# A fifteenth weight buffer loaded behind the gathers, a shorter router, and a first expert tile copied by two engines

## The chip, the cores and the metric

The kernel runs on one core of a Trainium2 chip, from one launch. The metric is the device time of one execution, in microseconds (us). The engines are TensorE (PE in the profile), VectorE (DVE), ScalarE (ACT), GpSimd (POOL) and SyncE (SP). SP and POOL issue the DMA transfers that are spoken of here. All tensors are float32.

## The reference, cut to what matters

One layer of a decoder over 520 tokens (512 of a prompt, 8 of a decoding batch), model width 1024. Four token mixers, gates and an output projection give `hres`; then a mixture of experts follows, and the change is there:

```python
def hier_moe(x, rg_w, rg_b, re_w, re_b, w1, w3, w2):
    pg = softmax(t @ rg_w + rg_b)              # 4 groups
    pg_top, g_idx = top_k(pg, 1)               # the best group
    le = (t @ re_w + re_b).reshape(-1, 4, 4)   # 4 experts in each
    le_sel = einsum('ng,nge->ne', g_oh, le)
    e_val, e_idx = top_k(le_sel, 2)            # the two best experts in it
    wts = softmax(e_val) * pg_top
    h = silu(t @ w1[e]) * (t @ w3[e]) * gate   # width 256, 16 experts
    return h @ w2[e]
y = hres + hier_moe(rms_norm(hres, norm2), ...)
```

## The kernel before

**Up to the router** (to about 609 us of the profile) the mixers, the merge and the output projection run on TensorE. They leave `hTr` (the sum `hres`, channels on partitions) and `hgT` (the same times the second norm's gain). The 520 tokens lie in `NB` = 5 blocks of `RB` = 104.

**The router** has PE form `ps[:, 4:6]` with router logits and mean squares (`logits`), summed over four row groups by the matmuls on `fold32` (L1156). `rows_of` (L1143) transposes a block of tokens back to rows, eight 128x128 transposes each: blocks of `hgT` are scaled by ACT (L1686, `tt_a`) and stored by SP to `scr_x` in DRAM (L543); blocks of `hTr` are copied by ACT (L1694) and stored by SP as the residual `out_y` (`residual`, L526). On DVE a chain of small instructions, each waiting for the one before (`link`), finds the best group and the two best experts (`sel`, 104x80 zeros and ones). PE ranks each token among those of its expert (L1165, L1167) and counts tokens of each expert (L1171). DVE turns ranks into places (`where`, `pos_f`) in tiles of 128 rows: 12 fixed tiles of 4 experts x 32 rows, and up to 10 overflow tiles. `steps` (L2424), POOL's `oh_tile` (L2680), `marks` (L2430) and `oh_row` (L2433) are one-hot operands with which PE (L1178, L1182) builds the table of token numbers, which DVE writes to `from_row` (L2444, semaphore `tab_ok`). A second table, of the weights, goes the same way (L2461, L1190, L1194, L2474, semaphore `g_ok`).

**The gathers**: POOL waits for all five `scr_x` stores (`xs_ok`) and for `tab_ok`, then gathers tiles 0, 1, 2 from DRAM by an indirect DMA each (L2686) into `xe` (tiles `cg`, `sgt`, `dqk`).

**The experts**: PE transposes a gathered tile in two halves of four 128x128 blocks (`rows_T`, L1204); ACT copies the first half from PSUM (`rows_copy`, L1699) and DVE the second (L2479), 512 columns each, into `xeT`. Then come the hidden products (L1215), 32 matmuls of 512 columns for a tile, and the output products (L1285). This runs in four quads of three tiles. `hidden_first` begins tile 0 of quad 0 by itself. POOL scatters results with indirect adds to `out_y` (L2691).

**The weights** of the experts are 48 parts of 1 MB (`weights(n)`), 12 for a quad: 8 for the hidden and 4 for the output products. They go through `STREAM` = 15 buffers: 14 whole ones (parts of `kv`, `br`, `sgd`, `qb`, `vtok`, `qk`, `tmp`, `xn`) and a fifteenth, number 14, made of four pieces (in `dv`, `vec`, `vtok`), filled by four DMAs of 256 KB (L513). SP's order is written by hand, and all of SP's DMAs are on one queue: parts 0 to 9 are issued during and after the output projection, part 14 right behind part 9, then the `scr_x` stores, the residual stores of blocks 0 to 2, those of blocks 3 and 4 (behind the landing of gather 0), parts 10 and 11 (behind gather 2), parts 12 and 13 (behind all residual stores), and then part by part as buffers come free. Part 14 is first read in quad 1.

**Who waits for whom around the change**: ACT is in order: five L1686 copies, a table load, an exponential (L1688, waits for `r1` 2), an exponential (L1690, waits for `r1` 3), five L1694 copies, then, behind `g_ok`, the copies of `rows_copy`. `r1` is counted up by DVE. In PE's order the last two `rows_of` and both table products stand ahead of `rows_T(0)`.

## Time and profile before

| | us |
|---|---|
| median of 3 runs | 791.31 |
| lowest, highest | 790.29, 791.31 |
| the profiled execution's own time | 790.43 |
| span of its instructions | 788.5 |
| PE busy | 762.8 (97%) |
| DVE, ACT, POOL busy | 382.4, 225.5, 294.9 |

The span runs from the first to the last instruction; the execution's own time is 1.9 us more. PE's busy time includes waits inside pipelined matmuls, so that 97% does not say that nothing else can end the time. The DMA engines moved 148.32 MB; in the last quarter of the span they are busy nearly all the time.

### The profile page before, as it was taken

The numbers are of one execution on the slowest core, as the hardware profiler recorded it, in microseconds if no ns is written. First come the engines' busy times: TensorE is split into PE (matmuls) and PEld (weight loads), VectorE is DVE, ScalarE is ACT, GpSimd is POOL, SyncE is SP. The second block draws the span as 40 slices with busy tenths as digits, with TensorE's granted clock in tenths as the row PEclk, the third lists the DMA queues.
The fourth block names the chain that finished last, engine by engine and source line by source line (L and its number), as shares of the span: only waits on it lengthen the run. The fifth ranks groups of instructions, "written<-read, shape, count | busy, mean of one in ns | idle before, by whom it ended". The sixth has DMA issues, their size and how long they took to land.

```text
span 788.5 us, 14312 instructions
## 1 busy us (share of the span) xinstructions
PE 762.8 (97%) x5277; PEld 545.0 (69%) x5277; DVE 382.4 (48%) x713; ACT 225.5 (29%) x436; POOL 294.9 (37%) x221
## 2 busy tenths in 40 slices
PE   8999999999999999999999999999999799999992
PEld 7887778676677888777767788888888634333330
DVE  4637777677497689543534113734533712031210
ACT  4131344342423454142414223322201512020100
POOL 0000331364553975255524554434250112332314
PEclk9999999999999999999999999999999999999996
DMA  9342662355665542245535453342761899999933
GB/s 363 119 162 82 204 195 86 85 159 168 184 178 188 169 137 66 80 150 175 174 122 174 122 190 141 100 159 69 267 267 51 310 337 410 371 389 370 384 116 50
DMA packets 72538, 148.32 MB, mean 188 GB/s; under 512 B 13335, under 2 KB 47144, under 8 KB 70420
## 3 DMA queue, kind: packets, MB, share of 16 engines
q1 hardware_dynamic: 65716, 135.43, 49.9%
q0 software_dynamic: 5920, 10.82, 5.6%
q10 hardware_dynamic: 832, 1.16, 0.5%
q8 instruction: 42, 0.69, 0.4%
q14 instruction: 28, 0.23, 0.1%
HBM read 137.71 MB, written 18.90 MB: 199 GB/s over the span
## 4 chain that ended last, share of the span: by engine, by line
PE 92%; DMA 3%; ACT 2%; DVE 1%; issue 1%; POOL 0%; SPq 0%; POOLq 0%; ACTq 0%
PE ps L874 23%; PE ps L608 17%; PE ps L1215 11%; PE ps L843 7%; PE ps L1120 6%; PE ps L1285 5%; PE ps L651 3%; PE ps L623 3%; PE ps L900 2%; PE ps L597 2%; PE ps L678 1%; PE ps L1204 1%; DMA scr_x<-cst 1%; PE ps L707 1%; PE ps L694 1%; DMA tmp<-in_xT 1%
## 5 line engine op out<-in xcount | busy, mean ns | idle before, releaser
L608 PE MATMUL ps<-xn,ring 128*128 128x268 f32 (+1 forms) x576 | 136.5, 391 | 0.2 <-ACT qk L1378 0.2
L608 PEld LDWEIGHTS ps<-xn,ring 128*128 128x128 f32 x576 | 106.9, 190 | 24.5 <-issue 4.2
L2576 POOL TENSOR_TENSOR kv<-kv,sgd 128x1024 f32<-128x1024 f32 (+1 forms) x32 | 80.4, 2526 | 98.8 <-DVE tmp L1848 51.7
L1530 ACT ACTIVATE sgt<-sgt,vec 128x260 f32<-128x260 f32 x60 | 30.1, 510 | 122.8 <-DVE sgt L2129 70.8
L2691 POOL DMA_INDIRECT out_y<-cst,gtab x24 | 37.3, 1555 | 70.9 <-DVE cst L2498 42.0
L843 PE MATMUL ps<-br,ring 128*128 128x260 f32 x256 | 61.0, 386 | 0.6 <-DVE sgt L2133 0.6
L874 PE MATMUL ps<-xn,ring 128*128 128x260 f32 x240 | 58.0, 385 | 0.0
L874 PE MATMUL ps<-xn,qb 128*128 128x260 f32 x240 | 57.6, 383 | 0.1
L843 PEld LDWEIGHTS ps<-br,ring 128*128 128x128 f32 x256 | 47.8, 190 | 11.2 <-issue 3.2
L1876 DVE TENSOR_REDUCE sgd<-kv 128x32 f32<-128x1024 f32 (+1 forms) x32 | 40.7, 1279 | 21.4 <-POOL kv L2576 21.4
L874 PEld LDWEIGHTS ps<-xn,qb 128*128 128x128 f32 x240 | 45.4, 190 | 7.4 <-issue 0.4
L874 PEld LDWEIGHTS ps<-xn,ring 128*128 128x128 f32 x240 | 45.0, 190 | 7.4 <-issue 0.4
L2485 DVE TENSOR_TENSOR ring<-ring,ps 128x256 f32<-128x256 f32 x12 | 5.1, 422 | 71.1 <-ACT ring L1705 71.1
L2120 DVE TENSOR_TENSOR sgt<-ps,sgt 128x260 f32<-128x260 f32 x15 | 6.4, 427 | 59.3 <-PE ps L874 59.3
L2620 POOL TENSOR_TENSOR qb<-qb,ring 128x512 f32<-128x512 f32 x15 | 19.1, 1277 | 40.6 <-PE ps L874 40.6
L2615 POOL TENSOR_TENSOR qb<-ring 128x512 f32<-128x512 f32 x15 | 19.6, 1306 | 36.1 <-PE ps L874 35.8
L2587 POOL TENSOR_TENSOR cst<-sgt,cst 128x520 f32<-128x520 f32 x16 | 20.6, 1288 | 27.7 <-ACTq L1540 27.7
L623 PE MATMUL ps<-kv,ring 128*128 128x268 f32 x128 | 29.9, 392 | 1.0 <-DMA ring<-in_w_in 0.6
L2627 POOL TENSOR_TENSOR qb<-ring,qb 128x512 f32<-128x512 f32 x15 | 19.8, 1323 | 27.0 <-PE ps L874 26.5
L1378 ACT ACTIVATE cst<-ps 128x520 f32<-128x520 f32 x32 | 19.3, 604 | 37.1 <-PE ps L843 37.0
L651 PE MATMUL ps<-ring,xn 128*128 128x128 f32 x256 | 29.7, 275 | 0.0
L651 PEld LDWEIGHTS ps<-ring,xn 128*128 128x128 f32 x256 | 29.1, 192 | 0.3 <-issue 0.2
(525 smaller groups left out, 1499.6 us busy)
## 6 DMA issues: line engine op xcount, KB each, us to landing
ring<-in_w_mg SPq DMA_DIRECT2D x32, 640.0 KB, 4.7
kv<-in_kc SPq DMA_DIRECT2D x128, 128.0 KB, 2.3
kv<-in_vc SPq DMA_DIRECT2D x128, 128.0 KB, 2.1
ring<-in_w_in SPq DMA_DIRECT2D x24, 512.0 KB, 5.0
kv<-in_w SPq DMA_DIRECT2D x8, 1024.0 KB, 13.1
br<-in_w SPq DMA_DIRECT2D x7, 1024.0 KB, 12.9
sgd<-in_w SPq DMA_DIRECT2D x6, 1024.0 KB, 14.4
qk<-in_w SPq DMA_DIRECT2D x6, 1024.0 KB, 11.0
```

Source lines behind the costliest of these rows:

```text
L608: mm = pe.matmul(ps[:, 2 * (t % 2) + h, 0:hw], wsl(c, k), xnv[:, k, col0 + h * hw:col0 + (h + 1) * hw], start=(k == 0), stop=(k == KT - 1))
L623: mm = pe.matmul(ps[:, EARLY[name] + h, 0:HT], wsl(c, k), xgv[:, k, h * HT:(h + 1) * HT], start=(k == 0), stop=(k == KT - 1))
L651: pe.matmul(ps[:, 2 * (t % 2), b * P:(b + 1) * P], xnv[:, k, b * P:(b + 1) * P], wsl(c, k), start=(k == 0), stop=(k == KT - 1))
L843: mm = pe.matmul(ps[:, bk + h, 0:HN], wsl(CAT[f"G{n}{m}"], KT + k), brv[:, BR[n] + k, h * HN:(h + 1) * HN], start=(k == 0), stop=(k == 1))
L874: mm = pe.matmul(ps[:, bk, 0:HN], w[:, k * P:(k + 1) * P], x, start=(k == 0), stop=(k == 3))
L1120: mm = pe.matmul(ps[:, bk, 0:HN], wk, x, start=(k == 0 and i in (1, 2, 5)), stop=(k == 3), skip_group_check=(i in (6, 7, 4, 3)))
L1215: mm = pe.matmul(ps[rows, i % ROUNDS, :], xeT[i % (2 * ROUNDS)][:, k, rows], slot[(i // ROUNDS * 12 + k - k % 2 + g // 2) % STREAM][2 * (g ...
L1285: mm = pe.matmul(ps[rows, LAST_OUT[r][n] if last else 6 + n, :], hT[r][:, f, rows], w[g][2 * f + n], start=(f == 0), stop=(f == 1), tile_p ...
L1530: act.activation(g, g, ACT.Sigmoid, bias=vv(V_BM + 8 * "ABCD".index(n) + m + i)).then_inc(g_a, 1)
L1876: dve.tensor_reduce(row, kb.rearrange("p s (m d) -> p s m d", d=32), X, ALU.add).then_inc(k_used, 1)
L2576: pool.tensor_tensor(kb, kb, qbc[:, b:b + 1, :].to_broadcast([P, HALF // 2 + (half and u), 256]), ALU.mult)\
L2691: pool.indirect_dma_start(out=o["y"], out_offset=on_rows(to), in_=rows.rearrange("p a n -> p (a n)"), in_offset=None, bounds_check=N - 1, ...
```

## The change

- SP: the four loads of part 14 move from in front of the `scr_x` stores to behind parts 12 and 13.
- PE: only four transposes of `rows_of(hgT, 0)` stand ahead of the L1156 products (`rows_half`), the other four behind them. The rank takes one matmul on running sums over blocks instead of four on single blocks; the count takes one instead of five.
- DVE: the bias is multiplied by the root and the logits stay unscaled; the two best experts are found with one comparison (`beaten` minus its transpose); a scan over 96 columns makes the block sums (`cum_b`); the overflow counts come from one scan over 64 columns (`cum_e`) instead of a sum, a scan over 16 and a difference. Places are integers, and `bitwise_and` with 127 takes the place of a sum over `steps` and a multiply-add. `oh_row` is made in three pieces (blocks 0-1, 2-3, 4), `marks` behind the first. Six instructions on the gate's weights, the last of which counts `r1` to 3, move from ahead of `rank` to behind `oh_row`; the expansion of the first choice (`outer(f1, ...)`) and two memsets move behind `tab_ok`. Three small instructions for constants are added at the masks, near 490 us.
- Tile 0: its first half is transposed into two PSUM banks, and ACT and DVE copy 256 columns each; PE waits for DVE's at k = 2. The banks of the following half tiles turn by one.

```diff
@@ SP
-            sp.wait_ge(outs, 16 * POOL_OUTS)
-            weights(STREAM - 1)
             for b in range(NB):
                 sp.wait_ge(tt_a, b + 1)
                 sp.dma_start(scr_x[b * RB:(b + 1) * RB, :], tk[b]).then_inc(xs_ok, 16)
...
             weights(12)
             weights(13)
+            sp.wait_ge(outs, 16 * POOL_OUTS)
+            weights(STREAM - 1)
@@ PE
-            for b in range(NB - 1):
-                mm = pe.matmul(rank[:, b + 1:, :], every[:, 0:RB], selm[:, b:b + 1, :].to_broadcast([RB, NB - 1 - b, NE]),
...
+            pe.wait_ge(sel_ok, 2)
+            pe.matmul(rank, every[:, 0:RB], cum_b[0:RB].rearrange("p e b -> p b e")[:, 0:NB, :], start=False, stop=True).then_inc(rank_ok[0], 1)
+            mm = pe.matmul(ps[:, 5, 0:NE], every, cum_b[0:RB, :, NB], start=True, stop=True)
@@ DVE
-            tt(ahead, to, of, ALU.is_gt)
-            link(tt(ties, to, of, ALU.is_equal))
-            link(tt(ties, ties, tri4[R].rearrange("p (e f) -> p e f", e=4).unsqueeze(1).to_broadcast([RB, NB, 4, 4]), ALU.mult))
-            link(tt(ahead, ahead, ties, ALU.add))
-            link(dve.tensor_reduce(r[9], ahead, X, ALU.add))
+            link(tt(beaten, to, of, ALU.is_gt))
+            link(tt(beaten, beaten, tri4[R].rearrange("p (e f) -> p e f", e=4).unsqueeze(1).to_broadcast([RB, NB, 4, 4]), ALU.mult))
+            link(tt(balance, beaten, beaten.rearrange("p b e f -> p b f e"), ALU.subtract))
+            link(dve.tensor_reduce(r[9], balance, X, ALU.add))
...
             outer(sel, r[18]).then_inc(sel_ok, 1)
+            dve.wait_ge(sel_ok, 1)
+            dve.tensor_tensor_scan(flat(cum_b[R]), flat(no_first[R]), flat(blocks[R]), 0.0, ALU.mult, ALU.add)\
+               .then_inc(sel_ok, 1)
...
-            link(dve.tensor_reduce(eov, over4, X, ALU.add))
-            link(dve.tensor_tensor_scan(eend, cst[:, C_ONE:C_ONE + NE], eov, 0.0, ALU.mult, ALU.add))
-            link(tt(edel, eend, eov, ALU.subtract))
+            link(dve.tensor_tensor_scan(cum_e[:, 1:], cst[:, C_ONE:C_ONE + 4 * NE], over4.rearrange("p e n -> p (e n)"), 0.0,
+                                        ALU.mult, ALU.add))
...
-            link(dve.tensor_reduce(tile_f[R, :], steps[R, :, 1:], X, ALU.add))
-            link(stt(row_f[R, :], tile_f[R, :], -float(P), pos_f[R, :], ALU.mult, ALU.add))
-            for b0, b1 in ((0, 3), (3, NB)):
+            link(ts(row_i[R, :], pos_f[R, :], P - 1, None, ALU.bitwise_and))
+            for b0, b1 in ((0, 2), (2, 4), (4, NB)):
...
+            tt(one[1][:, :, 0], one[1][:, :, 0], rstd2, ALU.mult).then_inc(r1, 1)
@@ ACT, DVE: tile 0
+            act.activation(xeT[0][:, 0:2, :].rearrange("p k n -> p (k n)"), ps[:, 3, 0:256], ACT.Copy).then_inc(m_ta, 1)
...
+            dve.tensor_copy(xeT[0][:, 2:4, :].rearrange("p k n -> p (k n)"), ps[:, 4, 256:512]).then_inc(m_td, 1)
```

On SP's queue, around the stores of `scr_x`, this stood before (tiles `dv`, `vec`, `vtok` of L513 are part 14, `qk` parts 8 and 9):

```order
L510 DMA qk<-in_w 128x2048 [waits op_mm]
L510 DMA qk<-in_w 128x2048
L513 DMA dv<-in_w 128x512 [waits outs]
L513 DMA dv<-in_w 128x512
L513 DMA vec<-in_w 128x512
L513 DMA vtok<-in_w 128x512
L543 DMA scr_x<-cg 104x1024 [waits tt_a]
L543 DMA scr_x<-sgt 104x1024 [waits tt_a]
L543 DMA scr_x<-dqk 104x1024 [waits tt_a]
L543 DMA scr_x<-cst 104x1024 [waits tt_a] x2
L526 DMA out_y<-xn 104x1024 [waits tt_a] x3
```

and from the residual stores on (tile `xn` of L515 is parts 12 and 13) this stands now:

```order
L531 DMA out_y<-xn 104x1024 [waits tt_a] x3
L531 DMA out_y<-xn 104x1024 [waits tt_a,m_xe0]
L531 DMA out_y<-bg 104x1024 [waits tt_a]
L515 DMA tmp<-in_w 128x2048 [waits m_xe2,tt_t]
L515 DMA tmp<-in_w 128x2048
L515 DMA xn<-in_w 128x2x1024 [waits y_out]
L515 DMA xn<-in_w 128x2x1024
L518 DMA dv<-in_w 128x512 [waits outs]
L518 DMA dv<-in_w 128x512
L518 DMA vec<-in_w 128x512
L518 DMA vtok<-in_w 128x512
L515 DMA kv<-in_w 128x2x1024 [waits m_use] x2
```

The four loads moved from in front of the `scr_x` stores to between parts 12/13 and part 15 (`kv`).

On DVE, from the first place (`steps`, 104x230) to the table of token numbers (`gtab`), before:

```order
L2423 TENSOR_TENSOR dr<-ea,dr 104x5 [waits dch]
L2424 TENSOR_TENSOR ring<-dr 104x230 [waits dch]
L2427 TENSOR_REDUCE dr<-ring 104x10 [waits idx2_ok]
L2428 SCALAR_TENSOR_TENSOR dr<-dr 104x10 [waits dch]
L2430 TENSOR_TENSOR ring<-ring,dr 104x10x22 [waits oh2_ok,dch]
L2433 TENSOR_TENSOR ring<-dr 104x2x384
L2433 TENSOR_TENSOR ring<-dr 104x2x256
L2439 COPY dr<-ps 64x128 [waits route_t]
L2444 TENSOR_SCALAR gtab<-ps 128x22 [waits route_t]
L2446 COPY dr<-ps 128x64 [waits route_t]
```

and now, `oh_row` in three pieces and the moved instructions behind them (tile `ea`):

```order
L2441 TENSOR_TENSOR ring<-dr 104x230 [waits dch]
L2443 TENSOR_SCALAR dr<-dr 104x10
L2446 TENSOR_TENSOR ring<-dr 104x2x256 [waits dch]
L2451 TENSOR_TENSOR ring<-ring,dr 104x10x22 [waits oh2_ok]
L2446 TENSOR_TENSOR ring<-dr 104x2x256
L2446 TENSOR_TENSOR ring<-dr 104x2x128
L2453 TENSOR_SCALAR ea<-ea 104x20
L2454 TENSOR_TENSOR ea<-ea 104x20
L2455 TENSOR_TENSOR ea<-ea 104x20 [waits dch]
L2456 TENSOR_TENSOR ea<-ea 104x20 [waits dch]
L2457 TENSOR_REDUCE ea<-ea 104x5 [waits dch]
L2458 TENSOR_TENSOR ea<-ea,small 104x5 [waits dch]
```

A sum and a multiply-add in front of `oh_row` became one small instruction that does not wait; the first `oh_row` piece no longer stands behind POOL's `oh2_ok`; six instructions stand between the last piece and the copy of the table (L2439 before).

On PE, from the choice (`sel_ok`) to the transposes of `hTr`, before:

```order
L1165 MATMUL ps<-dr,cst 104x80 [waits sel_ok]
L1167 MATMUL ps<-dr,cst 104x64
L1167 MATMUL ps<-dr,cst 104x48
L1167 MATMUL ps<-dr,cst 104x32
L1167 MATMUL ps<-dr,cst 104x16
L1171 MATMUL ps<-dr,cst 128x16 x5
L1143 MATMUL ps<-cst,tmp 104x128 [waits tt_a]
```

and now:

```order
L1146 MATMUL ps<-cst,xn 104x128 [waits tt_a]
L1146 MATMUL ps<-cst,xn 104x128 x7
L1176 MATMUL ps<-dr,cst 104x80 [waits sel_ok]
L1178 MATMUL ps<-ea,cst 104x80 [waits sel_ok]
L1179 MATMUL ps<-ea,cst 128x16
L1146 MATMUL ps<-cst,tmp 104x128 [waits tt_a]
```

Seven rows of rank and count products became three, the second of which waits for one more count of `sel_ok`.

## Rows read from the trace of the kernel before

**Rows 1.** The chain of waits, router and first tile: start us, us, what.

```profile
609.37 1.01 PE ps L1143 x8
...
616.96 9.02 DMA scr_x<-cst
...
626.85 4.75 DMA cg<-scr_x,gtab
...
632.46 0.61 ACT ring L1699
...
633.11 5.07 PE ps L1215 x32
...
763.40 10.48 PE ps L1285 x96
```

**Rows 2.** Timeline, PE: first and second tile's matmuls: start, us, engine, what.

```profile
633.11 3.35 PE L1215 MATMUL ps<-kv,ring 128*32 128x512 f32 x16 [0.26 <-ACT ring L1699]
...
639.13 1.92 PE L1215 MATMUL ps<-sgd,ring 128*32 128x512 f32 x16
```

**Rows 3.** Windows: us, PE busy, granted clock, DMA share, GB/s.

```profile
632.00:636.00 4.00, 3.74 (x24) 0.58 0.76 235
...
672.00:742.00 70.00, 70.00 (x644) 1.00 1.03 380
```

**Rows 4.** Timeline of DVE, router, to the end of both tables.

```profile
609.43 0.43 DVE L2351 COPY ea<-ps 128x260 f32<-128x260 f32 x1 [1.21 <-PE ps L1133]
...
615.33 0.24 DVE L2373 TENSOR_TENSOR dr<-ea 104x80 f32<-104x80 f32 x1
...
616.80 0.22 DVE L2405 TENSOR_SCALAR dr<-ps 104x80 f32<-104x80 f32 x1
...
618.20 0.22 DVE L2413 TENSOR_REDUCE dr<-dr 128x16 f32<-128x64 f32 x1
...
618.68 0.17 DVE L2415 TENSOR_TENSOR dr<-dr 128x16 f32<-128x16 f32 x1
...
620.54 0.40 DVE L2424 TENSOR_TENSOR ring<-dr 104x230 f32<-104x230 f32 x1
...
624.32 0.28 DVE L2439 COPY dr<-ps 64x128 f32<-64x128 f32 x1 [0.79 <-PE ps L1178]
...
625.09 0.18 DVE L2444 TENSOR_SCALAR gtab<-ps 128x22 int32<-128x22 f32 x1 [0.49 <-PE ps L1182]
...
630.48 0.18 DVE L2474 COPY dr<-ps 128x22 f32<-128x22 f32 x1 [0.49 <-PE ps L1194]
```

**Rows 5.** Groups of DVE instructions by shape: busy us, mean ns.

```profile
L2433 DVE TENSOR_TENSOR ring<-dr 104x512 f32<-104x512 f32 x1 | 0.7, 683 | 0.0
...
L1920 DVE TENSOR_TENSOR_SCAN cx<-br,qk 128x528 f32<-128x528 f32 x2 | 2.4, 1245 | 0.0
```

**Rows 6.** Timeline, POOL and DVE: one place at 314 us, one in the router.

```profile
314.32 1.33 POOL L2617 TENSOR_TENSOR ring<-ring 128x512 f32<-128x512 f32 x1
314.45 1.48 DVE L2052 TENSOR_TENSOR tmp<-tmp,dqk 128x256 f32<-128x256 f32 x1
...
621.02 0.55 POOL L2680 TENSOR_TENSOR ring<-ring 104x220 f32<-104x220 f32 x1 [13.52 <-DVE ring L2424]
```

**Rows 7.** Timeline, ACT: the second logit copy, the copies of `hTr` rows.

```profile
608.25 0.39 ACT L1677 ACTIVATE ea<-ps 128x260 f32<-128x260 f32 x1
...
618.77 2.85 ACT L1694 ACTIVATE xn<-ps 104x1024 f32<-104x1024 f32 x3 [0.20 <-PE ps L1143]
```

**Rows 8.** Timeline, SP's issues: the residual stores, the last weight part.

```profile
619.83 12.10 SPq L526 DMA_DIRECT2D out_y<-xn  x4
...
741.46 0.33 SPq L510 DMA_DIRECT2D br<-in_w  x1
```

**Rows 9.** DMA issues at 633 to 634 and 741 to 742 us: KB, us to landing.

```profile
cg<-scr_x,gtab POOLq DMA_INDIRECT x1, 9.8
...
br<-in_w SPq DMA_DIRECT2D x1, 1024.0 KB, 17.3
```

More of the change, by code:

```diff
@@ L1135, in logits, with rows_half @@
                     mm.then_inc(lg_t, 1)
+            def rows_half(src, b, n, h):
+                bk = (0, 2, 6)[n % 3]
+                for k in range(4 * h, 4 * h + 4):
+                    mm = pe.transpose(ps[0:RB, bk + h, (k % 4) * P:(k % 4 + 1) * P], src[:, k, b * RB:(b + 1) * RB], ident)
+                return mm
             def rows_of(src, b, n):
@@ L1140, in rows_of @@
                     pe.wait_ge(tt_a, n - 2)
-                bk = (0, 2, 6)[n % 3]
-                for k in range(KT):
-                    mm = pe.transpose(ps[0:RB, bk + k // 4, (k % 4) * P:(k % 4 + 1) * P], src[:, k, b * RB:(b + 1) * RB], ident)
-                mm.then_inc(tt_t, 1)
+                rows_half(src, b, n, 0)
+                rows_half(src, b, n, 1).then_inc(tt_t, 1)
             for j in range(KT // 2):
@@ L1151, in _ @@
             logits(1)
-            rows_of(hgT, 0, 0)
+            rows_half(hgT, 0, 0, 0)
             pe.wait_ge(lg_a, 1)
@@ L1165, in _ @@
             pe.matmul(rank, cst[0:RB, C_LT:C_LT + RB], selm, start=True, stop=False)
-            for b in range(NB - 1):
-                mm = pe.matmul(rank[:, b + 1:, :], every[:, 0:RB], selm[:, b:b + 1, :].to_broadcast([RB, NB - 1 - b, NE]),
-                               start=False, stop=(b == NB - 2))
-            mm.then_inc(rank_ok[0], 1)
-            for b in range(NB):
-                mm = pe.matmul(ps[:, 5, 0:NE], every, selm[:, b, :], start=(b == 0), stop=(b == NB - 1))
+            pe.wait_ge(sel_ok, 2)
+            pe.matmul(rank, every[:, 0:RB], cum_b[0:RB].rearrange("p e b -> p b e")[:, 0:NB, :], start=False, stop=True).then_inc(rank_ok[0], 1)
+            mm = pe.matmul(ps[:, 5, 0:NE], every, cum_b[0:RB, :, NB], start=True, stop=True)
             mm.then_inc(cnt_ok[0], 1)
@@ L1198, in rows_T @@
                 i, h = u // 2, u % 2
-                if u >= 3:
-                    pe.wait_ge(m_ta if u % 2 else m_td, (u - 3) // 2 + 1)
+                if u == 2:
+                    pe.wait_ge(m_ta, 1)
+                if u == 3:
+                    pe.wait_ge(m_td, 1)
+                if u == 4 or u > 4 and u % 2 == 0:
+                    pe.wait_ge(m_td, (u - 3) // 2 + 2)
+                if u > 4 and u % 2:
+                    pe.wait_ge(m_ta, (u - 3) // 2 + 1)
                 if h == 0:
@@ L1715, in out_copy @@
                 act.activation(yb[i % ROUNDS][:, 0, :], ps[:, LAST_OUT[i % ROUNDS][0] if last else 6, :], ACT.Copy, scale=g_w[:, i:i + 1]).then_inc(m_ya, 1)
-            for i in range(ROUNDS):
+            act.wait_ge(m_t, 1)
+            act.activation(xeT[0][:, 0:2, :].rearrange("p k n -> p (k n)"), ps[:, 3, 0:256], ACT.Copy).then_inc(m_ta, 1)
+            for i in range(1, ROUNDS):
                 rows_copy(i)
@@ L2399, in _ @@
-            for i in (15, 18):
-                dve.memset(r[i], 1.0)
-            fl = [v[R].rearrange("p b g e -> p b (g e)") for v in (f1, sel, at_slot, pos)]
+            beaten, balance = f1[R], f2[R]
+            link(tt(beaten, to, of, ALU.is_gt))
+            link(tt(beaten, beaten, tri4[R].rearrange("p (e f) -> p e f", e=4).unsqueeze(1).to_broadcast([RB, NB, 4, 4]), ALU.mult))
+            link(tt(balance, beaten, beaten.rearrange("p b e f -> p b f e"), ALU.subtract))
+            link(dve.tensor_reduce(r[9], balance, X, ALU.add))
@@ L2402, in _ @@
+            tt(r[0], r[0], rstd2.unsqueeze(2).to_broadcast([RB, NB, 4]), ALU.mult).then_inc(r1, 1)
+            dve.memset(cum_e[:, 0:1], 0.0)
+            fl = [v[R].rearrange("p b g e -> p b (g e)") for v in (f1, at_slot, pos)]
+            fl.insert(1, blocks[R, :, 1:].rearrange("p e b -> p b e"))
             dve.wait_ge(*rank_ok)
@@ L2435, in _ @@
                    each.unsqueeze(3).to_broadcast([RB, 2, b1 - b0, P]), ALU.is_equal).then_inc(oh_ok, 1)
+                if b0 == 0:
+                    dve.wait_ge(oh2_ok, 1)
+                    tt(marks[R, 0:2, :, 0:n_t], oh_tile[R], tokid[R].unsqueeze(1).unsqueeze(3).to_broadcast([RB, 2, NB, n_t]),
+                       ALU.mult).then_inc(oh_ok, 1)
+            ts(r[14], r[9], 1.0, None, ALU.is_equal)
+            link(tt(r[11], r[7], r[10], ALU.mult))
+            link(tt(r[13], r[7], r[14], ALU.mult))
+            link(tt(r[13], r[13], r[11], ALU.subtract))
+            link(dve.tensor_reduce(one[1], r[13], X, ALU.add))
+            tt(one[1][:, :, 0], one[1][:, :, 0], rstd2, ALU.mult).then_inc(r1, 1)
             def two_kinds(kind, bk):
@@ L2445, in _ @@
             dve.wait_ge(*tab_tt)
+            outer(f1, r[10])
+            for i in (15, 18):
+                dve.memset(r[i], 1.0)
             link(dve.tensor_copy(slots[:, 64:128], ps[:, 5, P:P + 64]))
@@ L2498, in out_copy @@
                 ts(yb[i % ROUNDS][:, 1, :], ps[:, LAST_OUT[i % ROUNDS][1] if last else 7, :], g_w[:, i:i + 1], None, ALU.mult).then_inc(m_yd, 1)
-            for i in range(ROUNDS):
+            dve.wait_ge(m_t, 1)
+            dve.tensor_copy(xeT[0][:, 2:4, :].rearrange("p k n -> p (k n)"), ps[:, 4, 256:512]).then_inc(m_td, 1)
+            dve.wait_ge(m_t, 2)
+            dve.tensor_copy(xeT[0][:, 4:8, :].rearrange("p k n -> p (k n)"), ps[:, 5, :]).then_inc(m_td, 1)
+            for i in range(1, ROUNDS):
                 rows_copy(i)
```

71 lines of the change are left out of this document (36 added, 35 removed).

## The prediction

> **What bounds the kernel now.** I read the chain of waits first. From 633.11 us on it is PE alone, tile after tile: the first tile's matmuls begin there, and the last output products begin at 763.40 [rows 1]. The windows agree: from 672 to 742 us PE is busy for all of its 70 us [rows 3]. Ahead of 633.11 the chain leaves PE. It runs through the last store of `scr_x`, whose transfer takes 9.02 us and is over at 616.96 + 9.02 = 625.98, through gather 0 (626.85, 4.75 us), and through ACT's copy of the first half tile (0.61 us) [rows 1]. So the change can win what it takes off the way from 609 to 633 us, and nothing behind it: the work there is the same. What ends the wait for the gathers last is close. The table of token numbers is written at 625.09 + 0.18 = 625.27 [rows 4], only 0.71 us ahead of the store. If the store goes faster by more than that, the DVE chain is the bound. Two things behind 633 matter too. The granted clock averages 0.58 from 632 to 636 us [rows 3], so part of this stretch was at 1.2 GHz and not at 2.4, after PE had done little but wait for the gather; the first 16 hidden matmuls took 3.35 us, against 1.92 for 16 of the second tile [rows 2]. And the DMA engines are full: share 1.03, 380 GB/s from 672 to 742 us [rows 3]. The last weight part is issued at 741.46 and lands 17.3 us later, at 758.8 [rows 8, 9]; PE wants it at 763.40 [rows 1]: a margin of 4.6 us.
>
> **Part 14 moved.** Its four DMAs stood just ahead of the stores on the same queue. Its 1.05 MB at 380 GB/s [rows 3] are 2.8 us. Taking them away lets the last store land up to 2.8 us earlier, plus 0.5 us for ACT's earlier copies (next part): 622.7. The ends are no gain at all (625.98, if the stores themselves are the limit) and 3.3 us. I take 622.7, since the stores of one queue are served in turn. The gain beyond 0.71 us is covered by the table.
>
> **The router, step by step (DVE, to `tab_ok`).**
> - PE starts the L1156 products behind four transposes instead of eight (8 take 1.01 us [rows 1]), but not before DVE's copy has ended at 609.86 [rows 4]: they start 0.47 us earlier.
> - The first bias instruction no longer waits for the reciprocal: 0.10 (a wait between two small instructions is some 0.03, and now they overlap).
> - The choice of two experts loses one 0.24 instruction that overlapped its neighbour: 0.17. Until `sel`: 0.74.
> - The rank. Before, `sel` ended at 615.33 + 0.24 = 615.57, and L2405, which waits for PE's rank, began at 616.80: 1.23 us [rows 4]. Now a scan over 96 columns comes first. A scan over 528 takes 1.245 us [rows 5], with some 0.15 fixed this is 2.07 ns a column, so 0.35 us. Behind it stand four small instructions and a memset, 0.65 us, longer than PE's one matmul. 1.02 against 1.23: 0.21. Until L2405: 0.95.
> - The counts. The sum (0.22) and the difference (0.17) go, with two waits of 0.03 [rows 4], the scan grows by 48 columns (0.10), and the short wait for PE's count (0.07) goes: 0.42. Until `steps`: 1.37.
> - From the start of `steps` (620.54) to the table's copy (624.32) it took 3.78 us [rows 4]. Now: 0.32 to the next issue, 0.17 + 0.03 for the mask, `oh_row` in pieces of 512, 512 and 256 columns (0.68, as the 512-column piece of before [rows 5], 0.68 and 0.42) with `marks` (0.39) between, less 0.21 of overlap, and then the six moved instructions, 0.93. Sum 3.41, a gain of 0.37. PE's last products, 0.7 us before, are behind the third piece alone and are hidden by the six.
> - A collision. POOL's `oh_tile` starts 0.08 us behind `steps` and takes 0.55 [rows 6]. Before, DVE was in a sum there; now it starts the first `oh_row` piece, a product of two operands in SBUF, 0.04 us behind POOL's start. At 314 us such an instruction of 256 columns, begun 0.13 us behind POOL's, took 1.48 us, where 512 columns alone take 0.68 [rows 6, 5]: it waited until POOL was through. Here it would end 0.38 us later. Ends 0 and 0.55; I take 0.38.
>
> Sum to `tab_ok`: 0.74 + 0.21 + 0.42 + 0.37 - 0.38 = 1.36 us, so it comes at 623.91, behind the store at 622.7. POOL is released at 623.91 and not at 625.98: 2.07 us earlier.
>
> The page "SBUF — State Buffer" of the Trainium skill (Who interferes with whom) says that the pair of ports shared by DVE and GpSimd is locked for a whole instruction, and that a `tensor_tensor` with both inputs in SBUF contends with GpSimd's reads. The row at 314 us agrees [rows 6]. By that rule the 0.38 is due, and without it the sum would be 1.74; this is a rule against this change's new order.
>
> **What the moved six delay.** The last of them counts `r1` to 3, on which ACT's second exponential waits, and behind it in ACT's order the five copies of `hTr` rows. They began at 618.77 [rows 7]; now at about 623.2. SP's residual stores 0 to 2, issued from 619.83 [rows 8], go out from about 624.2 to 626.2, and gather 0 starts at 624.8: they meet. Before, they had 7 us of lead. Beside residual stores and weight loads a gather took 9.8 us [rows 9], against 4.75 [rows 1]. Here only three stores of 0.43 MB, 1.1 us each at 380 GB/s, are in the way, the first ahead of the gather's data. The ends are 0 and 2.0 us; I take 0.7, since the gather gets its turns beside the stores. Gather 0 lands 2.07 - 0.7 = 1.37 us earlier, at 630.2. The fifth copy of ACT ends at 628.0 and is covered by the gather. So is the weight table: it was through at 630.66 [rows 4], now it is 1.36 us earlier less 0.28 for two memsets and an expansion, 629.6. That cover is 0.6 us thick, and if the gather is quick, this table bounds the gain.
>
> **Tile 0.** ACT copies 256 columns (0.39, as 260 at L1677 [rows 7]) instead of 512 (0.61 [rows 1]): 0.21. DVE's half is ready beside it, as PE asks for it eight matmuls later. The bank turn costs nothing. The constants near 490 us go beside waits of DVE: nothing.
>
> **The weight stream.** Part 14 now stands behind 12 and 13, where the DMA is full; each later part comes 2.8 us later relative to the stream. The stream begins about 1.1 us earlier (parts 10 and 11 wait for gather 2). The last part: 758.8 - 1.1 + 2.8 = 760.5, wanted at 763.4 - 1.6 = 761.8. Covered, with 1.3 us left.
>
> **Sum.** 1.37 + 0.21 = 1.58 us. The clock's stretch stays, as the pause ahead of the first tile has the same shape. Against the profiled execution: 790.43 - 1.6 = 788.8. That execution lies 0.88 under the median of three runs and 0.14 above the lowest; the mean of these four times is 790.8, and 790.8 - 1.6 = **789.2** is my forecast.
>
> **The rivals.**
> - *The residual stores eat it.* The gather meets all three stores, 2.0 us: the gain is 0.07 + 0.21 = 0.3, time 790.5. For it: the 9.8 us row. Against: less traffic is in the way.
> - *The stores of `scr_x` still end last*, at 625.5, because they and not part 14 are the limit; the change doesn't do what it says. The gain is 0.5 + 0.21 = 0.7, time 790.1. Against: four DMAs stand directly in front of them.
> - *The clock doesn't fall.* PE's last pause is a little shorter; then the first 16 matmuls win back 3.35 - 1.92 = 1.4 us [rows 2]: 787.8, or 787.4 with the gather free of the stores, and the weight stream's margin is then used up, so not less than 787.0.
> - *The weight stream ends the kernel: slower.* If parts 12 to 14 are held by the residual stores, on whose landing they wait, and come 4.4 us later than before, as those stores are issued, the last part lands at 758.8 + 2.8 + 4.4 = 766.0, and PE waits 766.0 - 763.4 = 2.6 us over before: 793.4. It decides from 4.6 us of lateness on. Against: stores 3 and 4, the last ones, wait for gather 0, which lands earlier; and the stream may make up for a late start while it waits for PE.
>
> **How the numbers follow.** Forecast 0.50; stores eat it 0.18; `scr_x` last 0.08; clock 0.18; stream 0.06. The range takes in all but the slow end and the far fast end: 787.0 to 790.9. A measurement can tell some 0.2%, 1.6 us, from no change, so the forecast stands on the border: I give half of it to each side. Faster: 0.25 + 0.18 and 0.05 for gathers that meet nothing, 0.48. Slower: 0.07. Same: 0.45.
>
> **What would show it.** The copy of the table near 623.0 and `gtab` near 623.7; the first `oh_row` piece over 1.0 us long beside POOL; the last `scr_x` store landed before `gtab`; ACT's `hTr` copies from 623.2 and the residual stores from 624.2; gather 0 in 5.4 us; the first hidden matmul near 631.5; no wait of PE behind it. I am wrong if gather 0 takes over 7 us, if PE waits for a weight part, or if the fall of the clock moves.

## The result and the profile after

The kernel after takes 795.33 us (median of 10 runs, 793.38 to 800.23), against 791.31 us before (10 runs, 789.92 to 792.86): a ratio of 1.0055, 95% interval 1.004 to 1.007. It is slower by 4 us where some 2 us faster were forecast (789.2), and it lies above the stated range of 787.0 to 790.9. Its profiled execution took 800.23 us, the longest of its ten, so sizes are read below from differences inside the profile and from the experiments, not from its total.

The router itself came out shorter, by about half of what was foreseen. The timeline of DVE (start us, us, line, what), followed by POOL's `oh_tile`; the first row answers to L2351 at 609.43 in [rows 4]:

```profile
611.97 0.43 DVE L2373 COPY ea<-ps 128x260 f32<-128x260 f32 x1 [1.21 <-PE ps L1138]
...
617.47 0.30 DVE L2394 TENSOR_TENSOR dr<-ea 104x80 f32<-104x80 f32 x1
617.80 0.36 DVE L2412 TENSOR_TENSOR_SCAN ea<-dr 104x96 f32<-104x96 f32 x1
...
618.76 0.24 DVE L2424 TENSOR_SCALAR dr<-ps 104x80 f32<-104x80 f32 x1
...
622.29 0.40 DVE L2441 TENSOR_TENSOR ring<-dr 104x230 f32<-104x230 int32 x1
...
622.80 1.07 DVE L2446 TENSOR_TENSOR ring<-dr 104x512 f32<-104x512 f32 x1
...
626.05 0.28 DVE L2462 COPY dr<-ps 64x128 f32<-64x128 f32 x1
627.04 0.18 DVE L2467 TENSOR_SCALAR gtab<-ps 128x22 int32<-128x22 f32 x1 [0.71 <-PE ps L1190]
```

```profile
622.77 0.55 POOL L2710 TENSOR_TENSOR ring<-ring 104x220 f32<-104x220 f32 x1 [12.72 <-DVE ring L2441]
```

Everything ahead of this copy came 2.54 us later in this profile (611.97 against 609.43), where the change has only three small instructions near 490 us. They need not be the reason: in the 13 profiles other than that of before, the second half of the logits starts anywhere from 607.95 to 609.94, and e2 and e9 below, which are without them, have 608.68 and 608.09. Take the 2.54 off: `sel` ends 0.34 us earlier than before, the rank's reader 0.58, `steps` 0.79, the table's copy 0.81, `gtab` 0.59.

Then the gain is lost. ACT (timeline) has its exponential only at 626.15, and SP (timeline) issues the residual stores from 627.30, against 618.77 and 619.83 in [rows 7, 8]:

```profile
626.15 0.22 ACT L1707 ACTIVATE ea<-ea 104x10 f32<-104x10 f32 x1 [5.30 <-DVE ea L2458]
626.27 2.84 ACT L1711 ACTIVATE xn<-ps 104x1024 f32<-104x1024 f32 x3
```

```profile
627.30 8.97 SPq L531 DMA_DIRECT2D out_y<-xn  x4
636.32 1.63 SPq L531 DMA_DIRECT2D out_y<-bg  x1
```

The chain of waits (start us, us, what), to be laid beside [rows 1], and PE's waits (us in total, times, longest):

```profile
628.18 7.77 DMA cg<-scr_x,gtab
636.09 1.94 PE ps L1219 x8
638.02 5.68 PE ps L1230 x32
...
747.27 23.94 DMA br<-in_w
771.56 12.24 PE ps L1302 x96
```

```profile
PE ps L1302 <- DMA br<-in_w: 2.6, 1, 2.6
PE ps L1219 <- DMA cg<-scr_x,gtab: 2.6, 1, 2.6
```

There are three losses. Gather 0 takes 7.77 us instead of 4.75. The first tile takes 5.68 us instead of 5.07, with its transposes also slow. And ahead of the last output products PE waits 2.6 us for the last weight part, which in the kernel before was there 4.6 us early. The windows (PE busy, PEld, DVE, ACT, POOL, granted clock, DMA share, GB/s) show the clock: 0.51 from 625 to 632 us, 0.50 from 636 to 642, which is the lower of the two levels, 1.2 GHz; before, it was there only within 632 to 636 (0.58 on average [rows 3]).

```profile
625.00:632.00 7.00, 6.47 (x43) 5.26 (x41) 5.67 (x31) 4.97 (x6) 3.21 (x3) 0.51 0.50 135
632.00:636.00 4.00, 1.11 (x14) 0.74 (x10) 0.88 (x5) 0.04 (x1) 0.12 (x1) 0.93 0.83 294
636.00:642.00 6.00, 5.92 (x28) 2.56 (x32) 1.12 (x2) 0.38 (x1) 1.00 (x1) 0.50 0.79 242
```

### The profile page after: what moved, and what is told of

It is laid out like the page before. It is cut to its first block, busy times and chain, and to the rows that moved or that the text cites. A ratio compares the mean times of both kernels' runs of the same rounds, so it can differ in the third digit from the quotient of the medians.

```text
span 798.3 us, 14290 instructions
## 1 busy us (share of the span) xinstructions
PE 770.5 (97%) x5263; PEld 550.5 (69%) x5263; DVE 384.0 (48%) x719; ACT 225.4 (28%) x436; POOL 294.4 (37%) x221
## 3 DMA queue, kind: packets, MB, share of 16 engines
q10 hardware_dynamic: 832, 1.16, 0.5%
## 4 chain that ended last, share of the span: by engine, by line
PE 86%; DMA 5%; DVE 3%; SPq 3%; issue 2%; ACT 1%; POOLq 0%; POOL 0%; DVEq 0%; ACTq 0%
PE ps L879 23%; PE ps L613 16%; PE ps L1230 7%; PE ps L848 7%; PE ps L1125 6%; PE ps L1302 4%; PE ps L656 3%; DMA br<-in_w 3%; PE ps L628 3%; PE ps L905 2%; PE ps L602 2%; SPq L515 2%; PE ps L683 1%; PE ps L1219 1%; PE ps L712 1%
```

## The experiments

Theory M: the kernel after loses by two edits. Moving the six DVE instructions makes ACT, and behind it SP's residual stores, so late that gather 0 meets them; and part 14's 1 MB makes the weight stream late at its end. The rivals are that one of the two is all, or that the router's new order costs in itself. This table holds all runs; its four right-hand columns are differences of starts in the profiles: from the second half of the logits (first L1133 product before, L1138 after; 607.10 and 609.64) to gather 0; gather 0's own time, to its landing or, where that is not recorded, to the issue of the residual store that waits for it; from the logits to the first hidden product; and from there to the last 96 output products. The kernel before was run beside each of them and had a median of 790.73 to 791.01.

| kernel | median us | ratio, 95% | logits to gather | gather | logits to hidden | hidden to outputs |
|---|---|---|---|---|---|---|
| before | 791.31 | 1 | 19.76 | 4.75 | 26.01 | 130.22 |
| after | 795.33 | 1.004 to 1.007 | 18.54 | 7.77 | 28.32 | 133.61 |
| e1, part 14 back | 794.75 | 1.003 to 1.006 | 19.01 | 9.01 | 30.02 | 129.98 |
| e2, before with part 14 moved | 794.78 | 1.002 to 1.006 | 19.15 | 4.60 | 25.26 | 131.89 |
| e3, exponential late | 793.07 | 1.000 to 1.005 | 18.29 | 4.80 | 24.41 | 130.41 |
| e4, both | 790.15 | 0.997 to 1.000 | 18.87 | 4.98 | 25.12 | 128.80 |
| e5, e4, part 14 behind `scr_x` | 793.54 | 1.001 to 1.003 | 18.94 | 7.67 | 28.62 | 130.38 |
| e7, e1, residual stores late | 795.60 | 1.004 to 1.007 | 19.11 | 4.53 | 24.94 | 133.23 |
| e8, e5 with filler | 792.85 | 1.001 to 1.003 | 18.29 | 8.48 | 28.07 | 130.49 |
| e9, before with filler | 790.30 | 0.998 to 1.001 | 19.13 | 4.90 | 25.89 | 128.80 |
| e10, e3, part 14 earlier | 791.58 | 1.000 to 1.003 | 18.86 | 4.75 | 24.91 | 131.47 |
| e11, e4, one store late | 789.82 | 0.998 to 1.000 | 19.09 | 4.76 | 25.15 | 128.80 |
| e12, e3, half of part 14 moved | 791.34 | 0.998 to 1.002 | 19.11 | 4.67 | 25.18 | 129.22 |
| e13, e1, the six back | 790.28 | 0.999 to 1.001 | 20.02 | 4.62 | 26.25 | 128.80 |

### Undoing each edit: e1 to e4

e1 is the kernel after, e2 the kernel before, each with part 14's place changed:

```diff
@@ e1 (e2 makes the opposite move in the kernel before)
+            sp.wait_ge(outs, 16 * POOL_OUTS)
+            weights(STREAM - 1)
             for b in range(NB):
                 sp.wait_ge(tt_a, b + 1)
@@
             weights(13)
-            sp.wait_ge(outs, 16 * POOL_OUTS)
-            weights(STREAM - 1)
@@ e3 (e4 has this and e1's edit)
-            act.wait_ge(r1, 3)
-            act.activation(rt[0:RB, 16:18, :, 0], ..., ACT.Exp).then_inc(r2, 1)
             for b in range(NB):
                 act.wait_ge(tt_t, NB + b + 1)
...
+                if b == 2:
+                    act.wait_ge(r1, 3)
+                    act.activation(rt[0:RB, 16:18, :, 0], ..., ACT.Exp).then_inc(r2, 1)
```

> The changed kernel with the four loads of weight part 14 back in front of the scr_x stores; router, copies and all else as changed. Theory M (the time is lost by three things: gather 0 meets the residual stores, 7.8 us in the profile of after against 4.75; the stream of weights is late by part 14, PE waits 2.6 us for the last part; TensorE's clock at 1.2 GHz for longer): the PE wait for the last part goes, gather 0 stays over 7 us; 792.5 to 793.5 us. Rival S (the stream of weights alone makes the kernel slower): all of the loss goes, 789 to 790.5. Rival R (the router's order alone): 795, no change.

> The kernel before with only part 14 moved behind parts 12 and 13. Theory M: the last scr_x store lands near 622.5 and gather 0 starts some 0.7 us earlier; the residual stores go out early as before, gather 0 takes 4.7 to 5.2 us; the stream's margin of 4.6 us shrinks by 2.8 and just holds, no wait of PE: 790 to 791.5. Rival S: PE waits for the last part, 793 or more.

> The changed kernel with ACT's second exponential (which waits for r1 3) behind the third copy of hTr rows instead of ahead of the first; nothing else. The residual stores 0 to 2 then go out near 620 us again. Theory M: gather 0 takes 4.5 to 5.2 us instead of 7.8, and starts as in after; the weight stream starts earlier too and PE's wait for the last part shrinks: 791 to 792.5. Rival S: gather 0 quicker, but PE waits for the last part by as much more; 794 to 795. If the residual stores do not matter, gather 0 stays over 7 us.

> The changed kernel with both: part 14 back in front of the scr_x stores, and ACT's second exponential behind the third copy. What is left of the change is the shorter router and the first tile's copies. The table of token numbers is then ready before the last scr_x store, which ends the wait again: theory M 789.8 to 790.8 (0.2 from the first tile's copy, 0.5 from ACT's earlier copies). Rival R: 793 or more.

Both edits cost, each alone: e2 is 3.8 us over the kernel before beside it (791.01), e1 4.6 us over e4, which differs from it by the exponential alone. With both undone, e4 is 0.9 us under the kernel before, and its interval ends just short of no change. Theory M had the causes and not the sizes: e4 fell into its range, e1 and e3 came 1.25 and 0.6 us above theirs, and e2 went as its rival S, since PE did wait for the last part. The two do not add up (after 795.33, e1 794.75), as each ends a different wait, and the weight stream, too, starts from the gathers. e3 shows what the forecast was after: its first hidden product comes 24.41 us behind the logits, 1.60 us earlier than before, and the last part takes it back (PE waits 1.5 us for it). The profiled executions of e2 and e3 took 792.71 and 791.48 us, 2.1 and 1.6 us less than their medians, so that the waits in the profiles need not be those of the median; no profile shows a slower execution of them. The chain of e2 and PE's wait in it:

```profile
742.76 22.71 DMA br<-in_w
765.82 10.54 PE ps L1285 x96
```

```profile
PE ps L1285 <- DMA br<-in_w: 1.3, 1, 1.3
```

The last part of e2 was issued 108.8 us behind its first hidden product, where it was 108.35 before; it landed at 131.53 against 125.67. That is 5.9 us later for 1.05 MB, of which 2.8 us were forecast. The landing scatters between kernels, though: with part 14 in front it is 127.33 in e9 (740.91 + 20.4) and 126.93 in e11 (740.64 + 20.0), and with part 14 behind it is 130.05 in e3 and 131.12 in e10. Like beside like, the move made it 4.2 to 5.9 us later (e2 less e9, e2 less the kernel before) and 3.1 to 4.2 (e3 and e10 less e11). The margin scatters as well: the outputs start 4.6 us behind the landing in the kernel before, but 1.5 us behind it in e9 and 1.9 in e11, whose first tile is quicker. The windows of the stream's end tell a part of the reason (columns as above); the first fence is the kernel before, the second e2, both cut at the same distances, in steps of 2.5 us from 120 us behind the first hidden product:

```profile
753.11:755.61 2.50, 2.50 (x28) 0.78 (x24) 0.00 (x0) 0.00 (x0) 1.23 (x1) 1.00 0.85 248
755.61:758.11 2.50, 2.50 (x28) 0.78 (x24) 0.00 (x0) 0.00 (x0) 0.00 (x0) 1.00 0.35 84
758.11:760.61 2.50, 2.50 (x32) 0.73 (x24) 0.00 (x0) 0.26 (x1) 0.00 (x0) 1.00 0.12 23
```

```profile
753.94:756.44 2.50, 2.50 (x28) 0.74 (x24) 0.00 (x0) 0.00 (x0) 0.79 (x1) 1.00 0.97 334
756.44:758.94 2.50, 2.50 (x28) 0.78 (x24) 0.00 (x0) 0.00 (x0) 0.00 (x0) 1.00 0.79 254
758.94:761.44 2.50, 2.50 (x28) 0.78 (x24) 0.00 (x0) 0.00 (x0) 0.00 (x0) 1.00 0.33 103
761.44:763.94 2.50, 2.24 (x20) 0.68 (x12) 1.21 (x4) 1.15 (x3) 0.00 (x0) 1.00 0.09 28
```

The share falls in the same way, 0.79 to 0.33 to 0.09, some 2.5 us later than before (0.85, 0.35, 0.12): the mean of the 16 DMA engines is late by the bytes, as forecast. But the part had not landed then. It landed at 765.47, and from 764.40 on, in e2, SP's queue moved this (DMA view: packets, MB, share of 16 engines):

```profile
q1 hardware_dynamic: 3, 0.02, 3.7%
```

One engine, busy all the time, would be 6.3% of the 16. From 762.40 on, SP's queue has 2.1, 4.0 and 3.7% in steps of about 1 us. So in its last 3 us the part waits for less than one engine's work, while the mean share has long fallen. In e2 this tail is longer than in the kernel before; in e9, with part 14 in front, it is there too. Which engines, and why these, the rows don't tell.

### Where part 14 can stand: e5, e10, e12

```diff
@@ e5: e4 with part 14 behind the scr_x stores
                 sp.dma_start(scr_x[b * RB:(b + 1) * RB, :], tk[b]).then_inc(xs_ok, 16)
+            sp.wait_ge(outs, 16 * POOL_OUTS)
+            weights(STREAM - 1)
             for b in range(3):
                 residual(b)
@@ e10: e3 with part 14 ahead of parts 10 and 11
+            sp.wait_ge(outs, 16 * POOL_OUTS)
+            weights(STREAM - 1)
             sp.wait_ge(tt_t, 2 * NB)
             sp.wait_ge(m_xe[ROUNDS - 1], 16)
             weights(10)
@@ e12: e3 with pieces 0 and 1 of part 14 ahead of scr_x, 2 and 3 behind part 13
+            weights(STREAM - 1, range(2))
...
+            weights(STREAM - 1, range(2, 4))
```

> The delayed exponential as in e3 and e4; part 14 is issued right behind the five scr_x stores, ahead of the residual stores, where the DMA engines were half idle in e3 (243 GB/s between 624 and 629 us). Theory P (the place matters: the bytes cost only where the DMA engines are full): the scr_x stores land some 2 us earlier than in e4, gather 0 starts at 626.9 to 627.3 (e4 627.68), the last weight part is not late, PE waits for no part at the end; 789.0 to 790.0 against e4's 790.15. Rival Q (the four loads meet gather 0 or the residual stores wherever they are put behind scr_x): gather 0 takes over 6 us, 791 to 793.

> e3 (delayed exponential) with part 14 issued behind the last two residual stores and ahead of parts 10 and 11, at some 633.3 us, where SP waits for gather 2 and the DMA engines are not full (213 to 292 GB/s from 629 to 639 us in e3). Theory E (what counts is the lateness of the stream, and this place is half free): the gather and the first hidden product as in e3 (first hidden product 24.4 us behind the router's start), the last part 1 to 2.5 us earlier than in e3, no wait of PE at the end: 789.0 to 790.2. Rival L (1 MB behind the gathers is late wherever it is put): PE waits 1 to 2 us for the last part as in e3 (793.07 us median): 791.5 to 793.5. Rival G (gathers 1 and 2 meet these loads, tile 1 is late): PE waits for gather 1, 791 to 793.

> e3 with two of part 14's four loads (0.5 MB) back in front of the scr_x stores, the other two behind parts 12 and 13. Theory D (in proportion): the last part lands 2.6 us later than in e4 instead of 5.3, PE has no wait or under 0.3 us for it, the scr_x stores land 1.4 us earlier than in e4: 789.2 to 790.2. Rival L (any load put there makes the stream late by the slowest engine's queue): PE waits over 1 us, 791.5 to 793.

e5 went as its rival Q: the stream is in time (the last part landed 6.0 us ahead of the outputs), but on SP the four issues, which took 0.4 to 1.3 us each, pushed the residual stores from 12.1 us behind the logits (620.95 in e4) to 14.9 (624.65), and gather 0 took 7.67 us. Its time is 0.5 us above that rival's range. e10 went as its rival L: the gather is as before, and PE waits 2.6 us for the last part, though its median is 1.5 us under e3's. e12 went as its theory for the stream: PE waits 0.3 us, and the last part lands 128.9 us behind the first hidden product. Its time, 791.34, missed the theory's 789.2 to 790.2 and is not under e4's: its executions scatter from 787.95 to 793.93, and the 0.7 us that its gather could come earlier was not there (19.11). No place behind the `scr_x` stores was found at which the 1 MB costs nothing; in front of them it delays the gather by 0.6 us (18.87 in e4, 18.29 in e3). PE's waits of e10 and e12:

```profile
PE ps L1302 <- DMA br<-in_w: 2.6, 1, 2.6
```

```profile
PE ps L1303 <- DVE cx L2518: 0.3, 1, 0.3
```

The second fence does not name the part: it had landed at 763.99, 0.35 us before the outputs' start, and the profile puts the wait down to DVE's copy of `cx`.

### The gather and the residual stores: e7, e11, e13

```diff
@@ e7: e1 with all residual stores behind gather 0
-            for b in range(3):
-                residual(b)
             sp.wait_ge(m_xe[0], 16)
-            for b in range(3, NB):
+            for b in range(NB):
                 residual(b)
@@ e11: e4 with the exponential one copy earlier
-                if b == 2:
+                if b == 1:
@@ e13: e1 with the six gate instructions (L2453 to L2458) ahead of the wait for the rank
+            ts(r[14], r[9], 1.0, None, ALU.is_equal)
...
+            tt(one[1][:, :, 0], one[1][:, :, 0], rstd2, ALU.mult).then_inc(r1, 1)
             dve.memset(cum_e[:, 0:1], 0.0)
```

> The kernel after with part 14 back in front (as e1, 794.75 us) and all five residual stores issued behind the landing of gather 0; ACT's order is left as in the kernel after. Theory M (the gather meets the three residual stores): gather 0 takes 4.7 to 5.3 us again, the first hidden product starts 2.5 to 3 us earlier than in e1 relative to the router, parts 12 and 13 come later but in time; 791.0 to 792.5. Rival R (it is ACT's lateness and the order of the router, not the stores): gather or first tile stay as late as in e1, 794 to 796. Rival S (the residual stores, now late, hold parts 12 and 13 and PE waits for the last part): gather short, but 793 to 795.

> e4 (790.15 us) with ACT's exponential one copy earlier, behind the second hTr copy: residual stores 0 and 1 keep their time, store 2 goes out only at about 626.5 us, 1.1 us ahead of gather 0. Theory T (each residual store close ahead of the gather costs its own transfer time of about 1.1 us): gather 0 takes 5.7 to 6.2 us, first hidden product 1 us later than in e4, 790.9 to 791.5. Rival O (one late store is enough, the gather queues behind the whole of it): gather 0 takes 7 us or more, 792 to 794. Rival Z (one store costs nothing): as e4.

> e1 (part 14 in front, 794.75 us) with the six instructions on the gate's weights back ahead of the wait for the rank, so that ACT's second exponential and its copies are not delayed; its place in ACT's order is left as it was. Theory N (moving the six bought nothing that reaches the end while part 14 stands in front of the scr_x stores, since the stores release the gather at about 18.9 us behind the router's start either way): gather 0 starts 18.8 to 19.3 us behind the router's start and takes 4.8 us, first hidden product at 25.0 to 25.5: 789.8 to 790.6, as e4 (790.15). Rival V (the moved six are worth their 0.93 us): the table and with it the gather come up to 0.9 us later than in e4: 790.8 to 791.4. Rival R (something else in the new router makes the gather late): gather 0 over 6 us, 793 or more.

e7 settles the first loss. ACT is as late as in e1, the router is the same, only the stores are out of the way, and gather 0 takes 4.53 us instead of 9.01. Its row among the DMA issues (KB are left out there, us to landing), and PE's wait:

```profile
cg<-scr_x,gtab POOLq DMA_INDIRECT x1, 4.5
```

```profile
PE ps L1300 <- DMA br<-in_w: 4.4, 1, 4.4
```

The time was not won, though: parts 10 to 13 now stand behind the late stores, the last part came late, and PE waited 4.4 us for it. This is what rival S of e7 said, whose range its 795.60 us still exceeds by 0.6, and it is the slower rival of the prediction, by this kernel's own price.

How the gather is held shows in the DMA view of its first 4 us in the kernel after, 628.18 to 632.18 (queue: packets, MB, share of 16 engines; q1 is SP's, q0 POOL's), and of the rest, to 635.95:

```profile
q1 hardware_dynamic: 218, 0.81, 72.2%
q0 software_dynamic: 32, 0.13, 16.5%
```

```profile
q0 software_dynamic: 263, 0.70, 50.3%
q1 hardware_dynamic: 122, 0.43, 32.6%
```

In e7 no byte moves in the first 1.8 us behind the gather's issue; with the engines free it would then have its 0.5 MB. So the shares of the first 4 us mislead, as the gather has nothing to move in almost half of them. From 629.98, 1.8 us behind the issue, to the landing the same view has:

```profile
q1 hardware_dynamic: 247, 0.87, 45.4%
q0 software_dynamic: 295, 0.83, 42.8%
```

The page "DMA: Bandwidth & Descriptors" of the Trainium skill (Queues, rings and completion order) says that a DMA engine with several queue rows to serve changes between them packet by packet. Shares of 45% and 43% (POOL's queue has the start of gather 1 in it) agree with that. What the gather meets are the bytes that SP's queue still has 1.8 us behind the gather's issue. In the kernel before, e2 to e4, e7 and e9 to e13 that is 0.05 MB at most up to the landing, and the gather takes 4.5 to 5.0 us, whatever was moved in the 1.8 us (0.43 MB in the kernel before, 0.59 in e4, none in e7). In the kernel after, e1, e5 and e8 it is 0.87, 0.74, 0.31 and 0.57 MB, and it takes 7.77, 9.01, 7.67 and 8.48 us. The bytes alone don't set the length: 0.31 MB are 0.8 us at 380 GB/s, an estimate, and cost e5 2.9. In e8 the end of the gather looks like that of the weight stream. It landed at 634.91, and from 634.00 to 634.91 only this moved, again the share of one engine:

```profile
q0 software_dynamic: 8, 0.02, 6.7%
```

e11 was meant to set the price of a single store: store 2 was issued at 626.23, 1.4 us ahead of the gather, stores 0 and 1 as early as in e4, and the gather took 4.76 us. So my theory T and its rival O fell, and Z held: one late store cost nothing. It was through in time, though: SP's queue moved 0.58 MB in the 1.8 us and 0.04 MB behind them, as in e4 (0.59 and 0.04). What one store costs whose bytes come later than that was not measured; three cost 3 us and more. The chain of e11 (first row the last store of `scr_x`, released by ACT and not by part 14's issue):

```profile
618.27 8.51 DMA scr_x<-cst
627.66 4.76 DMA cg<-scr_x,gtab
633.71 3.64 PE ps L1230 x32
...
762.58 10.48 PE ps L1302 x96
```

e13 shows what moving the six was worth. The gather starts 1.15 us later than in e4, the first hidden product 1.13 us later, and the median is 0.13 us higher (790.28), which these runs can't tell from nothing; nor can they exclude the 1.1 us, as e4's interval alone is 2.5 us wide. Of rival V the delay held, of theory N the time.

### The clock: e8, e9

```diff
@@ e8 in e5, e9 in the kernel before: products that nobody reads
             for b in range(3):
                 rows_of(hTr, b, NB + b)
+            pe.wait_ge(tt_a, NB + 1)
+            for _ in range(14):
+                pe.transpose(ps[:, 6, 0:P], ident, ident)
@@ ahead of rows_T(0)
+            for _ in range(12):
+                pe.transpose(ps[:, 3, 0:P], ident, ident)
```

> e5 with idle transposes on PE (14 between the rows of block 2 and the first table's products, 12 ahead of the first gathered tile), which nobody reads. Theory C (the granted clock falls when PE has done little in the router, and the stretch at 1.2 GHz costs): no row of the clock below 1.00 between 616 and 640 us, the transposes of the last two hTr blocks take 1.95 instead of 3.65 us, and the time is 0.3 to 1.2 us below e5. Rival N (the stretch lies where PE waits for others anyway): clock full, time within 0.3 us of e5. Rival F (the filler stands in the way of the tables): 0.3 us or more above e5.

> The kernel before with the same idle transposes. Theory C: the stretch at 1.2 GHz at 632.6 to 636.0 us is gone, the first 16 hidden products take 1.92 instead of 3.35 us, the stream's margin of 4.6 us shrinks to 3.2 and holds: 791.0 - 1.4 = 789.6 (789.2 to 790.2). Rival N: the clock falls as before or elsewhere, 790.7 to 791.5. Rival W (the weight stream takes the gain back at the end): PE waits for a part, 790.5 to 791.5.

In e9 the stretch at 1.2 GHz between the gather and the first tile is gone, and the first products run as those of the second tile do. PE's timeline:

```profile
631.26 1.53 PE L1200 MATMUL ps<-cst 128*128 128x128 f32 x12
632.63 1.04 PE L1210 MATMUL ps<-cst,cg 128*128 128x128 f32 x8
633.98 1.92 PE L1221 MATMUL ps<-kv,ring 128*32 128x512 f32 x16 [0.31 <-ACT ring L1705]
```

From the first hidden product to the outputs it is 128.80 us instead of 130.22, which is the 1.4 us expected. The twelve fillers end at 632.79, though, and gather 0 had landed at 632.13: they stood up to 0.5 us in the way. The time is 790.30, 0.1 above theory C's range and 0.65 us under the kernel before beside it, in an interval that holds no change. In e8 the transposes of the last two `hTr` blocks take 1.96 us, as expected, but the clock falls again at 636.3 us, just behind PE's wait of 2.4 us for the long gather (3.58 us for the first 16 products), where theory C had it full up to 640; the time is 0.7 us under e5, with overlapping runs. The same 128.80 stands for e4, e11 and e13 without a filler: there the granted clock is at 1.2 GHz from about 623.5 to 630.5, under PE's transposes, and full again at the first tile. In e3, e7, e10 and e12, too, the first 16 products take 1.92 us. In the kernel before and e2 the one stretch lies on the first tile; with the new router and no filler it comes at 622.9 to 626.2 us, under the tables and the transposes, and where PE then waits 2.6 to 4.1 us for a long gather (after, e1, e5) a second one lies on the first tile. Where the stretch comes down decides 1.4 us.

## Why the prediction was wrong

All three signs that it named came: gather 0 over 7 us, PE waiting for a weight part, and a fall of the clock in another place.

- **Until `sel`, 0.74 forecast, 0.34 measured.** The L1156 products (now L1166) started 0.22 us earlier against DVE's copy (612.54 against 611.97, before 610.22 against 609.43), not 0.47, and DVE's reciprocal only 0.16. The bias gave 0.16 for 0.10. Of the 0.17 for the removed instruction 0.02 came through, as L2407, which reads a transposed view, and the instruction that writes `sel` (L2394) take 0.30 each, not 0.24. **Rank**: 0.21 and 0.24 (0.58 less 0.34), right; the scan of 96 columns took 0.36 for 0.35. **Counts**: 0.42 and 0.21 (0.79 less 0.58): the scan of 64 is 0.29 as forecast, but three instructions on a transposed view, one of which writes integers (L2437 to L2439), are 0.05 to 0.06 longer each. **One-hots and collision**: -0.01 forecast, 0.02 measured. The first `oh_row` piece took 1.07 us for 0.68 + 0.38 = 1.06. The page "SBUF — State Buffer" of the Trainium skill (Who interferes with whom), by which such an instruction waits out POOL's, agrees with this row to 0.13 us: POOL is through at 623.32, and 0.68 behind that is an end at 624.00, where it was 623.87. Then 0.22 us were lost at L1190, at 1.2 GHz. In all the gather was released 1.21 us earlier, not 2.07; e3 and e8 have 1.47.
- **The `scr_x` stores**: right. Without part 14 in front the chain of the kernel after runs through DVE and not through them.
- **The residual stores: the step that failed first.** Their lateness was foreseen and put 0.5 us short (forecast 624.2; 627.30 less 2.54 is 624.76). The term was 0.7 us with an end at 2.0; it measured 7.77 - 4.75 = 3.0, and 4.3 in e1. I had taken the gather to have its turns beside the stores, at a small price. The turns it had, 43% to 45% from 629.98 on; the price was wrong. The 0.87 MB of SP's queue in that time are 2.3 us at 380 GB/s, an estimate, and gather 0 landed only when 0.83 MB of POOL's queue had moved, against 0.69 in the kernel before. The 9.8 us of [rows 9], a gather beside weight loads, was the nearer row, and I had set it aside for the smaller traffic. The fast cases, and the rival with 2.0 us, went with it.
- **The weight stream: the step that failed second.** "Covered, with 1.3 us left" took the last part to be late by its bytes, 2.8 us, out of a margin of 4.6 from a single profile. It was 3.1 to 5.9 us late, and in e9 and e11 the margin was 1.5 and 1.9. With all of part 14 behind part 13 or ahead of part 10 (after, e2, e3, e10), PE waited 1.3 to 2.6 us for the last part, each time. The slower rival named the wait, and that its 2.6 us is also what was measured is luck: it had parts 12 to 14 held by the residual stores for 4.4 us, but parts 12 and 13 were issued from 4.8 us behind the first hidden product (642.79), against 4.6 before (637.75). What was missed is that a part's lateness by bytes is a mean over 16 engines, while the part landed when the last of them was through. At 0.06 its chance was too low.
- **The clock: "the stretch stays" was wrong** in both directions. In the kernel after, it covers the transposes, the first tile and most of the router's end; the first 16 products took 3.64 us and the next 2.33, against 3.35 and 1.89 before. In e3, e4, e7 and e10 to e13 it missed the first tile, which is the gain of the third rival, though the clock did fall in them, only earlier.
- **Tile 0**: right. From its first transpose to the first hidden product it is 1.16 us in e4 (632.77 to 633.93) against 1.38 before; 0.22 for 0.21.
- **A slip in the sum of the third rival**: 787.8 with the gather free of the stores is 787.1, not 787.4. Nothing rests on it.

The 4 us of the medians are thus shown as: -0.9 for router and tile 0 (e4), +4.6 for the exponential ahead of the copies (e1 less e4), and 0.6 more for part 14 on top of that, which alone would be 2.9 (e3 less e4) to 3.8 (e2); the sum is 4.3, and the median of the kernel before alone differs by 0.3 between the groups of runs (791.31 and 791.01). Moving part 14 would have needed up to 6 us to spare in the stream, where there were 1.5 to 4.6.

## What to carry to other kernels

Before instructions are moved behind others, list every engine that waits for their last semaphore and what its queue holds next: here six instructions of 0.2 us on DVE delayed ACT, ACT delayed SP, and SP's stores, free before, fell on the one transfer that the kernel waits for. And a load that is moved into a full stream can be late at the far end by more than its bytes (here 3.1 to 5.9 us for 2.8); compare it with the measured landing of more than one profile, and not with a mean rate.

The best kernels of the study are e4 and e11, the change without part 14's move and with the exponential behind two or three copies: 790.15 and 789.82 us, 0.9 and 1.1 us under the kernel before beside them, intervals 0.9967 to 0.9998 and 0.9977 to 1.0001.
